# Four routing passes over the streamed weights, a ring of six gathered rows, and a front spread by TensorE time

## The reference, cut to what matters

```python
q = (xb @ w_q).reshape(blk, PEER_HEADS, 2, PEER_DKEY // 2)     # 8 heads, 2 halves of 128
s = jnp.einsum('nhcd,hckd->nhck', q, subkeys)                   # 128 keys for each half
s1, i1 = lax.top_k(s[:, :, 0], PEER_TOPK)                       # 16 best of each half
s2, i2 = lax.top_k(s[:, :, 1], PEER_TOPK)
cand = (s1[..., :, None] + s2[..., None, :]).reshape(blk, PEER_HEADS, 256)
top, ti = lax.top_k(cand, PEER_TOPK)                            # 16 best pairs
idx = i1[ti // 16] * 128 + i2[ti % 16]                          # an expert of 16384
g = softmax(top)
a = gelu(einsum('nhkd,nd->nhk', u_tab[idx], xb))                # gather a row of u, dot it with x
out = einsum('nhk,nhkd->nd', g * a, v_tab[idx])                 # gather a row of v, add it weighted
```

## Time and profile before

| | us |
|---|---|
| median of three runs | 3928.57 |
| the profiled execution | 3929.12 |
| its span | 3927.5 |
| first and last dot of the back | 902.2 and 3916.3 |

### The profile page before, as it was taken

The page is one execution under the profiler, slowest core; times in us unless marked ns, Lnnn a source line. Parts: engine busy times, 40 slices in busy tenths (PEclk is TensorE's granted clock), DMA queues, the critical chain, the costliest instruction groups (busy, mean ns, idle before and its releaser), DMA issues.

```text
span 3927.5 us, 33430 instructions
## 1 busy us (share of the span) xinstructions
PE 3116.0 (79%) x9089; PEld 1656.2 (42%) x9089; DVE 2581.0 (66%) x6288; ACT 1163.9 (30%) x2530; POOL 1308.2 (33%) x1145
## 2 busy tenths in 40 slices
PE   5999999776786788777789777798877778866767
PEld 3665556463343335333345333344533333532322
DVE  2432334228768766898765898865698776577874
ACT  1222232212432343222353322344222223322211
POOL 0000000003444433444443444433344443344443
PEclk9778877778898899988899988899998889988889
DMA  3010000089999999999999999998999998899998
GB/s 160 25 41 22 22 24 26 17 309 377 412 420 415 404 403 376 420 413 406 401 397 362 400 418 401 396 379 317 401 418 414 399 415 348 349 420 416 410 417 347
DMA packets 187364, 1267.87 MB, mean 323 GB/s; under 512 B 23381, under 2 KB 24238, under 8 KB 39606
## 3 DMA queue, kind: packets, MB, share of 16 engines
q0 software_dynamic: 159488, 1131.10, 71.1%
q1 hardware_dynamic: 25350, 122.09, 7.9%
q10 hardware_dynamic: 2352, 12.72, 0.8%
HBM read 1238.95 MB, written 26.88 MB: 322 GB/s over the span
## 4 chain that ended last, share of the span: by engine, by line
PE 33%; DMA 21%; DVE 13%; issue 7%; ACT 5%; POOL 1%; DVEq 0%; SPq 0%; ACTq 0%; POOLq 0%
PE ps_acc L1295 21%; DMA uv_ring<-in_peer_uv,expert_index 20%; DVE uv_ring L1493 5%; PE ps_scores L1270 4%; PE ps_scores L1238 3%; DVE v_sums L1501 2%; PE ps_scores L1151 2%; ACT coef_diag L1110 2%; PE ps_fox_o L1169 1%; DVE key_top_index L1383 1%; PE ps_turn L1162 1%; DVE key_scores_rest L1384 1%; ACT L1019 1%; PE ps_acc L1139 1%; PE ps_scores L1152 1%
## 5 line engine op out<-in xcount | busy, mean ns | idle before, releaser
L1295 PE MATMUL ps_acc<-uv_ring,coef_diag 128*128 128x512 f32 x3200 | 1736.0, 690 | 680.1 <-ACT coef_diag L1110 679.7
L983 POOL DMA_INDIRECT uv_ring<-in_peer_uv,expert_index x1056 | 1260.5, 1194 | 1756.9 <-PE ps_acc L1295 1623.1
L1493 DVE CUSTOM_DVE_ANT_0 uv_ring<-uv_ring,h_rows 128x1024 f32<-128x1024 f32 x1056 | 1286.9, 1221 | 309.5 <-DMA uv_ring<-in_peer_uv,expert_index 306.0
L1295 PEld LDWEIGHTS ps_acc<-uv_ring,coef_diag 128*128 128x128 f32 x3200 | 663.6, 219 | 1618.6 <-ACT coef_diag L1110 924.8
L1102 ACT ACTIVATE gelu_u_dot_h<-u_dot_h 128x2 f32<-128x2 f32 x528 | 107.3, 203 | 1370.2 <-DVE u_dot_h L1493 1368.7
L389 PE MATMUL ps_z<-w_in,x_T 128*128 128x512 f32 x864 | 397.6, 619 | 0.0
L1110 ACT ACTIVATE coef_diag<-ident_f,coefficients 128x128 f32<-128x128 f32 x768 | 279.1, 395 | 332.0 <-DVE coefficients L1485 331.6
L1501 DVE SCALAR_TENSOR_TENSOR v_sums<-uv_ring,coefficients,v_sums 128x1024 f32<-128x1024 f32 x256 | 327.6, 1280 | 0.0
L1270 PE MATMUL ps_scores<-weight_chunk,rows_T 128*128 128x256 f32 x1152 | 261.9, 381 | 0.7 <-issue 0.7
L389 PEld LDWEIGHTS ps_z<-w_in,x_T 128*128 128x128 f32 x864 | 169.2, 200 | 206.6 <-issue 206.6
L1270 PEld LDWEIGHTS ps_scores<-weight_chunk,rows_T 128*128 128x128 f32 x1152 | 220.1, 191 | 61.0 <-issue 34.3
(11 more groups left out here) (206 smaller groups left out, 2648.0 us busy)
## 6 DMA issues: line engine op xcount, KB each, us to landing
weight_chunk<-scratch_keys_w SPq DMA_DIRECT2D x48, 1024.0 KB, 9.1
weight_chunk<-in_w_out_chunks SPq DMA_DIRECT2D x24, 1024.0 KB, 13.3
uv_ring<-in_peer_uv,expert_index POOLq DMA_INDIRECT x1056, 11.8
w_in<-in_w_in SPq DMA_DIRECT2D x8, 1548.0 KB, 24.6
uv_ring<-in_w_peer_q_T SPq DMA_DIRECT2D x8, 1024.0 KB, 22.7
x_T<-in_x_T POOLq DMA_DIRECT2D x9, 512.0 KB, 3.8
x_rows<-in_x_rows POOLq DMA_DIRECT2D x9, 512.0 KB, 4.6
x_mid<-in_x_rows SPq DMA_DIRECT2D x9, 512.0 KB, 16.3
```

What stands on the lines that cost most here:

```text
L983: pool.indirect_dma_start(out=ring[:, s % RING, :], out_offset=None, in_=dram["uv"], in_offset=bass.IndirectOffsetOnAxis(ap=idx[:, t % IDX ...
L1295: mm = pe.matmul(acc[:, c, :], diag[:, r, :], ring[:, r, D + c * 512:D + (c + 1) * 512], start=first, stop=False, skip_group_check=True)
L1493: dve.tensor_tensor_reduce(out=ring[:, s % RING, 0:D], in0=ring[:, s % RING, 0:D], in1=h2[:, t % 2, :], scale=1.0, scalar=0.0, op0=ALU.mul ...
```

## The change

- **Batches.** Tiles are routed in four passes, [0], [1, 2], [3, 4, 5] and [6, 7, 8], in place of six; each pass streams the eight key chunks once. The product with `w_out` runs in five groups in place of six (the last pass has the groups [6, 7] and [8]). So 32 key chunks and 20 chunks of `w_out` are streamed in place of 48 and 24.
- **Ring.** `uv_ring` has six buffers in place of eight. The room goes to a third `x_mid` and `rows_T`; `h_rows` has one buffer in place of two, `candidates` and `candidates_rest` lie in `expert_pair_one_hot`, and `expert_index` has five buffers in place of four. The reopening of `h_rows` moves from four slots before a tile to its first slot. Of the eight heads' query weights at the start, the last two wait for a free buffer.
- **Plan.** A step of attention of tile t now counts (13 + 7.5 t) / 33, a column of the projection 3.5, a step of routing 0.45, and the plan moves evenly by that sum.
- **Vector adds.** Where a slot stands beside attention or projection, every pair gives one slot to DVE; beside routing it stays at every second pair. In sum 369 of 1056 slots.

The planner's numbers set where each part of the front stands among the 1056 slots:

| part | slots before | slots after |
|---|---|---|
| rest of route [0] | 0 to 40 | 0 to 30 |
| attend 1; 1, 2 | 41 to 73 | 31 to 65 |
| project and route [1]; [1, 2] | 74 to 83, 84 to 149 | 66 to 91, 92 to 190 |
| attend 2, 3; 3, 4, 5 | 150 to 215 | 191 to 301 |
| project and route [2, 3]; [3, 4, 5] | 216 to 231, 232 to 361 | 302 to 347, 348 to 498 |
| attend 4, 5; 6, 7 | 362 to 427 | 499 to 609 |
| project and route [4, 5]; project [6, 7] | 428 to 443, 444 to 573 | 610 to 644 |
| attend 6, 7; 8 | 574 to 639 | 645 to 707 |
| project and route [6, 7]; project [8] | 640 to 655, 656 to 823 | 708 to 725 |
| attend 8, project [8] | 824 to 856, 857 to 866 | |
| route [8]; [6, 7, 8] | 867 to 997 | 726 to 867, and its last unit at 948 to 1040 |

The diff, cut to its core (the SP program, the index helpers and the renamed arguments are left out):

```diff
-BATCHES = [[0], [1], [2, 3], [4, 5], [6, 7], [8]]
+BATCHES = [[[0]], [[1, 2]], [[3, 4, 5]], [[6, 7], [8]]]
...
-RING, GRP = 8, 2
+RING, GRP = 6, 2
...
-    for ts in BATCHES:
-        weight += [2] * (ATT_STEPS * len(ts) + out_steps(ts))
+    for groups in BATCHES:
+        for ts in groups:
+            for t in ts:
+                weight += [(13.0 + 7.5 * min(t, TILES - 0.5)) / ATT_STEPS] * ATT_STEPS
+            weight += [3.5] * (OUT_CH * len(ts)) + [1.5] * (out_steps(ts) - OUT_CH * len(ts))
+            due += [(len(weight), SLOTS * t - 24) for t in ts if t]
...
-        weight += [1] * route_steps(ts)
+        weight += [0.45] * route_steps(tiles)
...
 def on_vector(g):
...
-    return g % 2
+    return 1 if BESIDE[GRP * g + GRP] else g % 2
...
-    cand = sb("candidates", [P, TOPK, TOPK])
-    cand2 = sb("candidates_rest", [P, TOPK, TOPK])
+    cand, cand2 = hot[:, 0], hot[:, 1]
-    IDX = 4
+    IDX = 5
-    h2 = sb("h2_rows", [P, 2, D])
+    h2 = sb("h2_rows", [P, D])
...
                 for h in range(PH):
-                    sp.dma_start(ring[:, h, :], dram["w_qT"][h]).then_inc(wq_in[h], 16)
+                    if h >= RING:
+                        sp.wait_ge(f_mm, 4 * (h - RING + 1))
+                    sp.dma_start(ring[:, h % RING, :], dram["w_qT"][h]).then_inc(wq_in[h], 16)
...
-                if s == 0:
-                    reopen(0)
-                if i == SLOTS - 4 and t < TILES:
-                    reopen(t + 1)
+                if i == 0 and s < NS:
+                    reopen(t)
```

More of the change, by code:

```diff
@@ L629, with chunk_order, cols_before @@
 CHAIN_AT, EXP_AT = 4, 13
+def chunk_order():
+    order, out_at, keys_at = [], [], []
+    for bi, groups in enumerate(BATCHES):
+        for _ in groups:
+            gi = len(out_at)
+            out_at.append(len(order))
+            order += [("out", gi, c) for c in range(OUT_CH)]
+        keys_at.append(len(order))
+        order += [("keys", bi, j) for j in range(PH)]
+    return order, out_at, keys_at
+CHUNK_ORDER, OUT_AT, KEYS_AT = chunk_order()
 def units_before(bi):
-    return PH * sum(len(ts) for ts in BATCHES[:bi])
-def cols_before(bi):
-    return OUT_CH * sum(len(ts) for ts in BATCHES[:bi])
+    return PH * sum(len(ts) for ts in FLAT[:bi])
+def cols_before(gi):
+    return OUT_CH * sum(len(ts) for ts in GROUPS[:gi])
 def out_steps(ts):
@@ L712, in front_plan @@
     first = max(f for f, s in due if s <= margin + 4)
-    upto, f = [], first
+    upto, at_work = [], total[first]
     for s in range(NS):
[L715 to L725, removed]
+        ahead = [(total[g] - at_work) / (at - margin - s) for g, at in due if at - margin > s and total[g] > at_work]
+        at_work += max(ahead) if ahead else total[-1]
+        upto.append(max(f for f in range(len(total)) if total[f] <= at_work + 1e-6))
+    beside = [f < len(on_pe) and on_pe[f] for f in upto]
+    return first, upto, len(weight), beside
+PROLOGUE, UPTO, FRONT, BESIDE = front_plan()
 def on_vector(g):
@@ L924, in chunk @@
             if n >= WBUF:
[L925 to L928, removed]
-                else:
[L930 to L939, removed]
+                was, owner, part = CHUNK_ORDER[n - WBUF]
+                if was == "out":
+                    sp.wait_ge(y_mm, cols_before(owner) + (part + 1) * len(GROUPS[owner]))
+                else:
+                    sp.wait_ge(s_mm, units_before(owner) + (part + 1) * len(FLAT[owner]))
+            if kind == "keys" and at == 0:
+                sp.wait_ge(f_st[c % 2], 16 * (c // 2 + 1))
+            sp.dma_start(wb[b][:], dram["w_out"][c] if kind == "out" else dram["keys_w"][c]).then_inc(wb_in[b], 16)
+        loaded = 0
+        for bi, groups in enumerate(BATCHES):
+            for t in groups[0]:
+                keys_queries(t)
+                mix_rows(t)
+                x_rows(t)
+            if TILES in groups[0]:
+                past()
             if bi == 0:
@@ L1088, in front @@
         def front():
-            for bi, ts in enumerate(BATCHES):
-                for t in ts:
-                    yield from attend(t)
-                yield from project(bi, ts)
-                yield from route(bi, ts)
+            for bi, groups in enumerate(BATCHES):
+                for ts in groups:
+                    for t in ts:
+                        yield from attend(t)
+                    yield from project(GROUP[ts[0]], ts)
+                yield from route(bi, FLAT[bi])
         def back():
@@ L1259, in route @@
                     j, i = divmod(m, n)
[L1260 removed]
+                    chunk = KEYS_AT[bi] + j
                     if i == 0:
@@ L1342, in project @@
                     c, i = divmod(step - 1, n)
[L1343 removed]
+                    dve.wait_ge(y_mm, cols_before(gi) + step)
+                    bi, place = PLACE[ts[i]]
                     if c == 0:
[L1345 to L1346 removed]
+                        dve.wait_ge(xr_in[place], 16 * sum(len(us) > place for us in FLAT[:bi + 1]))
+                    half = xr[place][:, c * CW:(c + 1) * CW]
                     bank = 512 * ((step - 1) % 3)
```

160 lines of the change are left out of this document (93 added, 67 removed).

## The result

| | us |
|---|---|
| before, median of these runs | 3927.07 |
| after, median of four (4174.49 to 4179.23) | 4177.89 |
| ratio, 95% interval | 1.063 (1.061 to 1.065) |
| profiled span after | 4172.9 |
| first and last dot after | 901.2 and 4163.3 |

The change makes the kernel 251 us slower. The forecast was 3960, the range 3870 to 4050. The back takes 4163.3 - 901.2 = 3262.1 us in place of 3014.1, 248 us more; what lies ahead of it has not moved.

A forecast was written before the change was run, and what follows sets the result against it. The second part was taken as near a transfer bound, with dips where PE is full beside attention. Its terms, 105 + 1196 + 1744 = 3045 us against 3014, add 31 to 3929.12: 3960 us, range 3870 to 4050.

The forecast's parts named there:

- first 31 slots: Start of the back, with what is left of route [0], some five units: 105 us.
- 392 slots beside routing: Back slots beside routing: DVE's work and waits set 3.05 us a slot, 1196 us; DMA would need about 2.65.
- other 632: Slots outside routing: DMA is the bound, floor 2.73 us a slot; taken at 2.76, 1744 us.
- the ring of six: Six gather buffers at 2.75 us a slot: a 16.5 us round leaves 8.9 us to land; 2.76 taken.
- a straight line: Slots outside routing: DMA share drawn between two windows by gathers in flight, 0.945 at 3.2, giving 2.89 us a slot.
- the hold: Time from a gather's landing to the next issue into its buffer, with the back alone: 7.6 us.
- The comparison with the shortest landing: Ring of six: 8.9 us to land against the shortest 5.5 leaves room, so the ring costs nothing: 2.73 us a slot.
- its end from above: Beside routing: PE's shorter lead in scores adds 0.8 us of waiting a unit, giving 3.18 us a slot.
- Beside attention: Attend stretches: PE falls to 1.8 us a slot, near 65%, no longer the bound; DVE's 1.95 us is hidden; DMA is next.
- The weights: Streamed key and `w_out` chunks: 21 MB less, 50 us at 416 GB/s, worth that only where DMA is the bound.
- GpSimd held by DVE: Rival, chance 0.10: denser DVE work lengthens gather issues beside attention by 0.5 us, 53 us over the forecast, 4013 us.
- the starved ring: Rival, chance 0.12: all six buffers wait together at times; 3.18 us a slot beside routing, 2.89 elsewhere, 4093 us.

The follow-up runs named there:

- e1: The kernel before with a ring of six buffers in place of eight and nothing else changed; 4157 us, 1.061 of the kernel before.
- e3: The changed kernel with a ring of seven buffers in place of six; 4032 us, 1.026 of the kernel before.
- e11: The kernel of e9 with a ring of six buffers in place of eight; 4077 us.
- e5: The changed kernel with eight buffers, DVE's routing chain and the exponential four front steps later behind PE's scores (chain at step 8, not 4); 3938 us.
- e2: The changed kernel with a ring of eight buffers in place of six; 3994 us, 1.0175 of the kernel before.
- e9: The changed kernel with eight buffers, the later chain of e5 and no vector adds beside routing; 3837 us, 0.977 of the kernel before.
- e10: The kernel of e9 with the six old passes in place of four; 3845 us, 0.980 of the kernel before.
- e4: The changed kernel with eight buffers and the six old passes, so the new plan alone; 3925 us, 0.9998 of the kernel before.

## Why the prediction was wrong

The back took 3262 us, the forecast had 3045. The first 31 slots took 105.5 us, as the sum had it. The 392 slots beside routing took 1265 us (319, 493 and 453), the forecast 1196: 69 more. The other 632 took 1891, the forecast 1744: 147 more. So the 248 us are the sum's own 31 plus 69 plus 147 and rounding.

**The step that failed is the ring of six.** The prediction worked out both ends for it: a floor of 2.73 us a slot, if 8.9 us to land leave room enough over the shortest landing, and 2.89, from a straight line through the shares of two windows with 2.8 and 3.7 in flight. It took 2.76, "near the free end", with the reason that PE's bursts made the window with 2.8 look worse than a short ring would. Measured were 2.99 us a slot over these 632 slots, and e1 to e3 put that on the ring alone: with eight buffers the same slots take 2.73, exactly the floor, 1726 us.

The term that was mis-sized is the hold. The prediction took 7.6 us from landing to the next issue, read with the back alone, and used it for all 632 slots. From the traces of the changed kernel, a buffer is held 7.6 us in the mean from slot 868 on, as it said, but 9.2 us in the slots before that outside routing, where PE and DVE also have attention and projection to do. Over the 632 slots the hold is 8.75 us and the landing 9.19 in the mean: together 17.94 us, over six buffers 2.99 us a slot. The prediction had 7.6 + 8.9 = 16.5. So most of the error is the hold, 1.15 us of 1.4.

The comparison with the shortest landing failed too, with the back alone, where the hold was right. At 2.56 us a slot six buffers leave 15.4 - 7.6 = 7.8 us to land. That is more than 2 us over the shortest landing and it did not suffice: the landing took 8.8 us and the slots 2.74 to 2.80. In e11, where from slot 948 on the hold of 6.9 us left 8.5, the rate was full. The shortest of 1056 landings says nothing of how many gathers must be under way.

The straight line, the other end, used the engines' busy share, and the share hides the loss. The rates of the same two windows, 351 GB/s at 2.8 in flight and 407 at 3.7, give 376 GB/s at 3.2, and 1.136 MB a slot (the gather and its 0.087 MB of the rest) at that rate take 3.02 us, where 2.99 was measured. That it comes so close is partly luck, as PE too held the first of the two windows: with the back alone 3.2 in flight gave 393 GB/s.

The times of all 1056 gathers show the same. I set each one's issue against the landing of the one before it; the difference is the lead. Worked out from the traces:

```
lead, us        changed kernel: count, us to the     before: count, us to the
                landing after the one before         landing after the one before
under 2         71, 5.0                              18, 6.9
2 to 4          179, 3.3                             36, 3.7
4 to 5          185, 3.3                             53, 3.1
5 to 6          166, 2.8                             62, 2.7
6 to 9          390, 2.7                             356, 2.8
over 9          64, 3.2                              530, 2.7
```

The times are means. A gather issued 5 us or more ahead mostly lands 2.7 to 2.8 us after the one before; with 2 to 5 us it comes 3.1 to 3.7 us after, in both kernels, and with less than 2 us later still. Of 1055 gathers 435 had less than 5 us in the changed kernel, 107 before. (The 64 of the changed kernel with over 9 us took 3.2 in the mean and 2.5 in the median.)

**Beside routing** the forecast was 3.05 and gave 3.18 as its end from above, for the reason that PE's lead of four steps shrinks from 5.5 to 4.7 us. Measured were 3.20 in route [3, 4, 5] with eight buffers and 3.26 with six. The mechanism was named and its size was right (2.2 us of waiting for scores a unit, 1.1 before); the value chosen, 3.05, left it out. This is the second step that failed. e5 shows it: with twice the lead the wait is gone. With eight buffers the routing slots take 1242 us, 46 over the forecast, which with six becomes 69.

**Beside attention** the step held: PE fell to 71% (65% forecast), and with eight buffers DMA is near full there, 411 GB/s from 2426 to 2730 us of e2. **The weights** were right in bytes and wrong in worth: e9 is 8 us faster than e10, which has six passes, at the edge of the noise, and e2 is 69 us slower than e4. **GpSimd held by DVE** did not come: beside attend 6, 7 the issue of a gather takes 942 ns in the median, 937 before, far from the 1.2 us that was its sign.

The rival that came true is the starved ring, to which I gave 0.12: 4093 forecast for it, 4178 measured. Its price was low mostly because it took 2.89 us for the 632 slots, which is 64 of the 85 us. The formula that the prediction set beside this step, 2.0 us plus bytes at 436 GB/s in the Trainium skill's DMA: Bandwidth & Descriptors, section Anatomy of one DMA, gives an estimate of 4.4 us for a gather. The shortest here took 5.3 us, and 7.8 us of room were not enough for the full rate with the back alone. The measurement decides: here the formula did not serve to size a ring.

## What to carry to other kernels

A ring of buffers has a round: the time from issue to landing plus the time a buffer is held until its next issue. The number of buffers over that round is the rate. Read both parts in every kind of stretch, not in the calmest one, since the hold was 7.6 us with the back alone and 9.2 beside attention. The room to land is not compared with the shortest landing, but with the landing time at which a window still had its full rate, here 8.5 us. And fullness is read from the GB/s, not from the engines' busy share, which was 0.98 at 92% of the rate. A plan that makes one stretch lighter makes another denser; before spreading work off a full engine, look how full the engine of the other stretch is, here VectorE at 91%. And where a producer and a consumer stand a fixed number of steps apart, a denser plan shortens that distance in time.

## What the hardware showed unexpectedly

One gather of 1 MiB lands 5.3 us after issue at the least, and the engines move it in 2.5 us, so that two or three would seem to cover the latency. With the back alone, 3.1 in flight gave 384 GB/s (e1), 3.2 gave 381 and 393 (the changed kernel), 3.3 gave 400 and 416 (e11), 3.9 gave 419 (e3), and 6.5/3.83 = 1.7, with four buffers, gave 277. Between 384 and 419 GB/s the busy share of the DMA engines moved only from 0.98 to 1.01.
